# The last attention group of a hybrid decoder trunk in another order: output projections ahead of the new rows' steps, first normalisation chunk ahead of the last heads' work

## The reference, cut to what matters

```python
# layer 0, for the 1024 prompt rows and the 8 sample rows
q, k, v = split(x @ w_qkv); q, k = rope(q), rope(k)
s = q k^T / 8, window of 128 back, with one sink per head
o = softmax_with_sink(s) v
x = layer_norm(ALPHA * x + o @ w_o, ln_mix_g[0], ln_mix_b[0])
u = x @ ffn_w_in[0]                      # and so on: the FFN of layer 0
# layer_norm: mu = mean(x); var = mean((x - mu)^2)
#             (x - mu) * rsqrt(var + eps) * g + b
```

## Time and profile before

| | |
|---|---|
| median of three runs | 2870.3 us (2869.7 to 2871.86) |
| the profiled execution's own time | 2871.64 us |
| its span, first to last instruction | 2869.8 us |
| PE busy | 2810.4 us (98%) |
| DVE, ACT, POOL busy | 1482.6, 899.0, 579.8 us |
| mean granted TensorE clock | 0.991 of full |

### The profile page before, as it was taken

How to read it: one execution, slowest core, us unless ns; L and a number is a source line. 1 busy time by engine, 2 the same in 40 slices (tenths; PEclk the granted TensorE clock), 3 DMA queues, 4 the chain that set the end, 5 groups by cost and what they waited for, 6 DMA issues and landing times.

```text
span 2869.8 us, 44638 instructions
## 1 busy us (share of the span) xinstructions
PE 2810.4 (98%) x18308; PEld 2704.3 (94%) x18308; DVE 1482.6 (52%) x2974; ACT 899.0 (31%) x1690; POOL 579.8 (20%) x505
## 2 busy tenths in 40 slices
PE   8999989999999999999999999999999999999996
PEld 7888879999999999999999999899999999999996
DVE  6556576444444444714445454365765444444446
ACT  5445454221111122422343433422252221222223
POOL 3334351000000002402223232111330000000004
PEclk9999999999999999999999999999999999999998
DMA  4210111111111112234566665776402111111101
GB/s 134 79 46 17 30 46 45 45 45 45 52 52 45 45 45 65 68 114 147 187 192 198 184 191 180 245 244 191 139 30 74 45 45 58 46 45 45 45 25 59
DMA packets 193434, 260.51 MB, mean 91 GB/s; under 512 B 29200, under 2 KB 151696, under 8 KB 193200
## 3 DMA queue, kind: packets, MB, share of 16 engines
q1 hardware_dynamic: 128336, 196.16, 21.8%
q10 hardware_dynamic: 64896, 61.50, 6.3%
HBM read 191.50 MB, written 68.20 MB: 90 GB/s over the span
## 4 chain that ended last, share of the span: by engine, by line
PE 91%; DVE 4%; ACT 2%; issue 1%; POOL 1%; DMA 1%; SPq 0%; ACTq 0%; DVEq 0%; POOLq 0%
PE bank L493 28%; PE bank L495 28%; PE bank L494 28%; PE bank L628 1%; PE bank L650 1%; ACT y L1046 1%; PE bank L955 1%; PE bank L908 1%; PE bank L640 0%; PE bank L917 0%; DVE bank L1525 0%; PE bank L902 0%; DMA xl<-scratch_heads_lo 0%; PE bank L605 0%; ACT xh L1050 0%
## 5 line engine op out<-in xcount | busy, mean ns | idle before, releaser
L493 PE MATMUL bank<-xh,wh 128*128 128x344 f32 x3600 | 1162.2, 323 | 6.5 <-DMA xl<-scratch_heads_lo 4.0
L495 PE MATMUL bank<-xh,wl 128*128 128x344 f32 x3600 | 1152.2, 320 | 0.0
L494 PE MATMUL bank<-xl,wh 128*128 128x344 f32 x3600 | 1151.4, 320 | 0.0
L493 PEld LDWEIGHTS bank<-xh,wh 128*128 128x128 f32 x3600 | 678.1, 188 | 21.9 <-issue 14.1
L494 PEld LDWEIGHTS bank<-xl,wh 128*128 128x128 f32 x3600 | 677.6, 188 | 4.8
L495 PEld LDWEIGHTS bank<-xh,wl 128*128 128x128 f32 x3600 | 678.3, 188 | 0.0
L1503 DVE TENSOR_TENSOR y<-bank,y 128x344 f32<-128x344 f32 x576 | 290.1, 514 | 219.4 <-PE bank L495 218.8
L2156 POOL TENSOR_TENSOR f_hl<-f_cv,f_hh 128x344 fp32r<-128x344 f32 x132 | 123.0, 932 | 1265.6 <-ACT f_hh L1198 1265.6
L493 PE MATMUL bank<-f_hh,wh 128*128 128x344 f32 x1056 | 340.2, 322 | 0.0
L495 PE MATMUL bank<-f_hh,wl 128*128 128x344 f32 x1056 | 337.7, 320 | 0.0
L494 PE MATMUL bank<-f_hl,wh 128*128 128x344 f32 x1056 | 337.4, 320 | 0.0
(11 more groups left out here) (230 smaller groups left out, 3417.3 us busy)
## 6 DMA issues: line engine op xcount, KB each, us to landing
raw<-in_w SPq DMA_DIRECT2D x216, 512.0 KB, 3.7
scratch_qkvg<-p_plain ACTq DMA_DIRECT2D x96, 172.0 KB, 2.8
r_s<-in_state_in SPq DMA_DIRECT2D x32, 512.0 KB, 3.7
out_state_s<-r_s ACTq DMA_DIRECT2D x32, 512.0 KB, 5.7
scratch_qkvg<-p_rot ACTq DMA_DIRECT2D x24, 344.0 KB, 3.1
xh<-scratch_heads_hi SPq DMA_DIRECT2D x12, 688.0 KB, 8.9
xl<-scratch_heads_lo SPq DMA_DIRECT2D x12, 688.0 KB, 10.4
r_cxq<-scratch_qkvg SPq DMA_DIRECT2D x32, 256.0 KB, 5.7
```

Of the source, the lines that this page charges most:

```text
L493: pe.matmul(out, ah, bh, start=(k == 0), stop=False)
L494: pe.matmul(out, ah, bl, start=False, stop=False)
L495: mm = pe.matmul(out, al, bh, start=False, stop=(k == n - 1))
```

## The change

In the last group only:

- PE: jobs 0 to 3 are issued in the loop ahead of the sample rows' projection (`project(8)`), jobs 4 and 5 between `turn(7)` and `values(4)`, jobs 6 and 7 ahead of `turn(8)`. `mean(0)` stands ahead of job 8, `var(0)` behind job 13, `mean(1)` still behind job 19.
- DVE: `centre(0)`, `sum2(0)`, `inverse_root(0)`, `scale(0)` move ahead of the last `inverse`, of `heads_lo(6)`, of `sample_probs_copy` and of `heads_lo(7)`; the adds follow the jobs.
- ACT: `squares(0)` moves ahead of `heads_hi(6)`; a one-element Sqrt behind `sample_exp` loads the table early; `root(0)` comes ahead of the slabs' splits; `normal(0, ...)` stands inside the group, around `sample_heads_hi`. The order of slab splits is now: 20 behind `root(0)`, 21 behind `heads_hi(7)`, 22 and 23 behind `normal(0, 1)`.
- POOL: the sums of chunk 0 go between the `probs`; its queue behind that is as before.
- The PSUM banks of the jobs from 8 on are 0, 1 and 3 in turn; the sample rows' scores move from bank 3 to bank 4. In SBUF a gap of 1152 words a partition moves ahead of `a_t1` to behind `a_t2`, so that the squares and sums lie free of them.

```diff
@@ def job_order() @@
-        jobs += [("qkv", g, b) for b in range(NB + 1)] + [("ao", g, q) for q in range(24)]
+        n = 4 if g == NG - 1 else 0
+        jobs += [("qkv", g, b) for b in range(NB)] + [("ao", g, q) for q in range(n)]
+        jobs += [("qkv", g, NB)] + [("ao", g, q) for q in range(n, 24)]
@@ PSUM bank of job q @@
+    if q < 8:
+        return q % 2
+    return (0, 1, 3)[(q - 8) % 3] if g == NG - 1 else (0, 1, 3, 4)[q % 4]
@@ tensor_engine: project, down @@
+            if last and b == NB:
+                pe.wait_ge(S["yadd"], 24 * g + 3)
...
+                if last and q in (0, 1, 4):
+                    pe.wait_ge(T["rope_t"], (NB + 1) * g + (NB + 1 if q == 4 else NB - 1 + q))
+                if last and q == 10:
+                    pe.wait_ge(S["n_cent"], 1)
@@ tensor_engine: attention @@
                 turn(t - 1)
+            if last and t == NB:
+                down(4, 6)
             if t >= 4:
                 values(t - 4)
             if t >= 3:
                 turn_probs(t - 3)
+            if last and t == NB - 1:
+                down(0, 4)
+        if last:
+            down(6, 8)
+            turn(NB)
+            values(NB - 3)
+            scores(NB - 1)
+            turn_probs(NB - 2)
+            pe.wait_ge(T["shifted"], GH * NB * (g + 1))
+            mean(0)
+            down(8, 10)
+            sample_scores()
+            values(NB - 2)
+            sample_turn()
+            down(10, 12)
+            turn_probs(NB - 1)
+            down(12, 14)
+            var(0)
+            values(NB - 1)
+            sample_turn_probs()
+            down(14, 16)
+            sample_values()
+            down(16, 20)
+            mean(1)
+            down(20, 24)
+            return
@@ scalar_engine: attention @@
+            if last and t == NB + 1:
+                pt_in(t - 3)
             if t >= 2:
                 exps(t - 2)
-            if t >= 3:
+            if t >= 3 and not (last and t == NB + 1):
                 pt_in(t - 3)
...
         if last:
+            act.wait_ge(T["expd"], NB * (g + 1))
             squares(0)
+            heads_hi(NB - 2)
+            sample_exp()
+            act.activation(K.warm[:, :], K.eps[:, :], ACT.Sqrt)
+            pt_in(NB - 1)
+            act.wait_ge(S["g_in"], 64)
+            root(0)
             split_next(1)
+            heads_hi(NB - 1)
+            split_next(1)
+            normal(0, 0)
+            sample_heads_hi()
+            normal(0, 1)
+            split_next(2)
@@ scalar_engine, behind the groups @@
-    act.wait_ge(S["g_in"], 64)
-    root(0)
-    normal(0, 0)
-    normal(0, 1)
     squares(1)
@@ vector_engine: attention @@
+            if last and t == NB - 1:
+                add_y(0, 4)
+        if last:
+            add_y(4, 6)
+            inverse(NB - 2)
+            add_y(6, 8)
+            t_lo(NB)
+            heads_lo(NB - 3)
+            shift(NB - 1)
+            centre(0)
+            inverse(NB - 1)
+            add_y(8, 10)
+            sample_copy()
+            sample_shift()
+            sum2(0)
+            add_y(10, 12)
+            heads_lo(NB - 2)
+            sample_probs()
+            add_y(12, 13)
+            inverse_root(0)
+            scale(0)
+            sample_probs_copy()
+            heads_lo(NB - 1)
+            add_y(13, 16)
+            sample_heads()
+            sample_heads_lo()
+            normal_lo(0, (0,))
+            add_y(16, 18)
+            normal_lo(0, (1,))
+            add_y(18, 20)
+            centre(1)
+            add_y(20, 24)
+            sum2(1)
+            return
@@ pool_engine: attention @@
             if t >= 3:
+                if t == NB + 1 and g == NG - 1:
+                    sums(key, 0, 0, 4, 6)
                 if t == NB + 2 and g == NG - 1:
-                    sums(key, 0, 0, 1, 4)
+                    sums(key, 0, 0, 6, KT)
                 probs(t - 3)
             if t <= NB:
                 add_rope(t)
+            if t == NB and g == NG - 1:
+                sums(key, 0, 0, 1, 4)
         if g < NG - 1:
...
         else:
-            sums(key, 0, 0, 4, KT)
             for s in range(20, 23):
                 split_lo(s)
             sums(key, 0, 1, 1, KT)
```

More of the change, by code:

```diff
@@ L201, with att_bank @@
 EV = evac_table()
+def att_bank(g, q):
+    if q < 8:
+        return q % 2
+    return (0, 1, 3)[(q - 8) % 3] if g == NG - 1 else (0, 1, 3, 4)[q % 4]
 def bank_table():
@@ L208, in bank_table @@
         kind = key[0]
-        if kind == "qkv" or (kind == "ao" and key[1:] < (NG - 1, 16)):
+        if kind == "qkv" or (kind == "ao" and key[1:] < (NG - 1, 8)):
             continue
         if kind == "ao":
-            b = (0, 1, 5)[key[2] % 3]
+            b = att_bank(key[1], key[2])
         elif kind == "up":
@@ L309, in last_columns @@
     return slice(2 * CH + part.start, 2 * CH + part.stop), part
[L312 to L316, removed]
 def att_before(g, q):
@@ L404, in build @@
         K.same = sb("same", [32, NS])
-        sb("a_gap", [P, 1152])
         K.a_t1 = sb("a_t1", [P, 2, 320])
         K.a_t2 = sb("a_t2", [P, 2, 320])
+        sb("a_gap", [P, 1152])
         K.a_sm = sb("a_sm", [P, GH, 2 * W])
@@ L659, in sample_scores @@
             for b in range(NS):
-                pe.matmul(bank[3][:, b:32:NS], K.a_kc[:, b, :], K.a_sq[:, 0:4, b], start=True, stop=True)
-            pe.matmul(bank[4][0:32, 0:NS], K.a_sq[:, 0:4, :], K.a_sq[:, 4, :], start=True, stop=True).then_inc(T["s_sc"], 1)
+                pe.matmul(bank[4][:, b:32:NS], K.a_kc[:, b, :], K.a_sq[:, 0:4, b], start=True, stop=True)
+            pe.matmul(bank[4][0:32, 32:32 + NS], K.a_sq[:, 0:4, :], K.a_sq[:, 4, :], start=True, stop=True).then_inc(T["s_sc"], 1)
         def sample_turn():
@@ L720, in attention @@
         sample_turn()
-        if last:
-            mean(0)
         down(8, 12)
@@ L727, in attention @@
         sample_values()
[L728 to L735, removed]
+        down(14, 24)
     def ffn_up(L, t, kind, ch):
@@ L1154, in attention, with sample_exp, sample_heads_hi @@
         act.dma_start(A["vwin_s"][:, W - 1, g, :], K.a_vs[:, :]).then_inc(T["kv_out"], 16)
[L1155 to L1165, removed]
+        def sample_exp():
+            act.wait_ge(T["s_mx"], 3 * g + 3)
+            act.activation(K.a_sp[:, :], bank[2][0:32, 0:W + 1], ACT.Exp, bias=K.a_sst[:, 2:3], scale=HD ** -0.5,
+                           accum_out=K.a_sst[:, 4:5])
+            act.activation(K.a_sst[:, 5:6], K.a_sst[:, 3:4], ACT.Exp).then_inc(T["s_ex"], 1)
+        def sample_heads_hi():
+            act.wait_ge(T["s_of"], 2 * g + 2)
+            act.activation(K.a_oh[:, :, SEQ:TOK], K.a_of[:, :, :], ACT.Copy).then_inc(T["s_oh"], 1)
         if last:
+            act.wait_ge(T["expd"], NB * (g + 1))
             squares(0)
-        act.wait_ge(T["s_of"], 2 * g + 2)
-        act.activation(K.a_oh[:, :, SEQ:TOK], K.a_of[:, :, :], ACT.Copy).then_inc(T["s_oh"], 1)
-        if last:
-            split_next(1)
-        else:
+            heads_hi(NB - 2)
[4 more added lines that the diff above has]
+            root(0)
+            split_next(1)
+            heads_hi(NB - 1)
[4 more added lines that the diff above has]
+            split_next(2)
+        else:
+            split_next(1)
+            heads_hi(NB - 2)
+            pt_in(NB - 1)
+            split_next(1)
+            sample_exp()
+            heads_hi(NB - 1)
+            split_next(1)
+            sample_heads_hi()
             act.wait_ge(S["jobs"], J["ao", g, 23])
@@ L1617, in sample_copy @@
             dve.wait_ge(T["s_sc"], g + 1)
-            dve.tensor_copy(K.a_ss[:, :], bank[3][:, 0:32]).then_inc(T["s_scc"], 1)
-            dve.tensor_tensor(K.a_new[:, 0:NS], bank[4][0:32, 0:NS], K.same[:, :], ALU.mult).then_inc(T["s_scc"], 1)
+            dve.tensor_copy(K.a_ss[:, :], bank[4][:, 0:32]).then_inc(T["s_scc"], 1)
+            dve.tensor_tensor(K.a_new[:, 0:NS], bank[4][0:32, 32:32 + NS], K.same[:, :], ALU.mult).then_inc(T["s_scc"], 1)
             dve.wait_ge(T["s_scc"], 3 * g + 2)
@@ L1693, in attention @@
         add_y(10, 12)
-        if last:
-            centre(0)
         heads_lo(NB - 1)
@@ L1700, in attention @@
         sample_heads_lo()
[L1701 to L1714, removed]
+        add_y(14, 24)
     def conv(L, t, ch):
```

## The result

The changed kernel takes 2874.26 us (median of 18 runs, 2872.25 to 2876.66), the kernel before 2870.23 (18 runs beside them): a ratio of 1.0015, 95% interval 1.0009 to 1.0021. It is 4.0 us slower, inside the range and within 0.2%, but on the slower side of no change: the interval excludes one. The prediction had 2871.7.

A forecast was written before the change was run, and what follows sets the result against it. PE, busy 98% of the span, was taken as the bound, with some 20 us winnable at most. Earlier chunk 0 work, offset by a new wait at mean(1), left var(1) 1.4 later: 2870.3 + 1.4 = 2871.7 us, range 2866.0 to 2878.0.

The forecast's parts named there:

- The bound, the place and the mechanism: PE-bound; at mean(1), PE waits 7 to 10 us for POOL's sums, held behind slab 22's split after normal(0,1).
- The early part: Last group up to mean(0): two new PE waits of 1.7 us each, yet mean(0) at 368.0 against 371.93.
- wait 1.1 us at job 13: Chunk 0: job 13 waits about 1.1 us for add 10, behind sum2, before var(0) runs to 380.65.
- wait 2.7 for the copy and 2.0 for the sample heads: Ahead of job 16, PE waits for DVE's steps behind scale(0); job 16 starts at 390.3.
- The new wait's size: At mean(1): slab 22's low part ends at 397.1, seven sums take 7.2; PE waits 7 to 10 us.
- the contention of the two engines: At sum2(1): DVE and POOL share SBUF interfaces, so 3.6 us; without it, var(1) ready 1.1 us sooner on DVE's side.
- From mean(1) to var(1): Half to all of jobs 20 to 23 run at low clock; FFN starts 411.4 to 412.8, var(1) 415.2 to 416.6.
- the +1.4: At var(1): it comes at 415.9 against 414.47, 1.4 us later, and the end moves by as much.
- no idle time that matters: PE behind the FFN's first var, in the kernel before: nothing there changes, so the end moves as var(1) does.
- The faster one: Wait at mean(1) absent or short: var(1) at about 408, 6.5 us sooner, 2863.8 us; chance 0.10.
- The slower one: Clock low for over 11 us after the wait at mean(1): 6.4 us, 2876.7 us; chance 0.15.
- The parts that I costed at nothing: Table load behind sample_exp, banks 0, 1, 3, the moved SBUF gap, slab loads, stores: no cost, apart from waits at jobs 13 and 23.

The follow-up runs named there:

- POOL's order: Changed kernel with POOL's sums of chunk 1 moved ahead of the low part of slab 22: 2864.72 us, ratio 0.9982 to the kernel before.
- ACT's order: Changed kernel with ACT splitting slab 22 right behind slab 21, ahead of normal(0,0): 2867.82 us, ratio 0.9994 to the kernel before.
- the cause alone: Kernel before with only ACT's splits of slabs 22 and 23 moved behind normal(0,1): 2886.77 us in one execution.
- the run with the extra matmuls: Changed kernel with 48 unread matmuls into free bank 7 ahead of mean(1), keeping PE busy: 2871.11 us, ratio 1.0004 to the kernel before.
- the first experiment: Changed kernel with POOL's sums of chunk 1 moved ahead of slab 22's low part: 2864.72 us, ratio 0.9982 to the kernel before.
- taking the 0.70 away: Changed kernel with POOL's chunk 1 sums ahead of slab 22, plus banks 1, 0, 3 in turn from job 8: 2864.77 us.
- the first try for a better order: The reordered-sums kernel with banks 1, 0, 3, plus sample rows' steps ahead of scale(0) and normal(0,0), and POOL's sums split: 2865.54 us, ratio 0.9989.
- the run of the table load: Kernel before with only a one-element Sqrt added behind sample_exp, loading the table early: 2870.04 us, ratio 1.0001.

## Why the prediction was right

**The bound, the place and the mechanism** were as put: mean(1) after 9.65 us of idle time that POOL ended (6 to 11 forecast), POOL idle 7.50 us ahead of its third low part (over 6), mean(0) and var(0) 3.4 and 10.3 us sooner, no table load ahead of the root, var(1) at 418.08, 0.1 outside the 413 to 418 I gave. POOL's order, ACT's order and the cause alone (9.5 and 6.4 us less than the changed kernel, 16.8 more than before) show the mechanism from both sides.

**The early part.** New waits of 1.67 and 1.91 for the 1.7 and 1.7 forecast. One step failed: I let jobs 10 to 13 run at full clock and had PE wait 1.1 us at job 13. The window at 374 us has the clock at 0.57 with no wait in it, behind the two short waits; what brings it the last section takes up. PE itself was late, there was no wait, and var(0) came at 380.81 for my 379.2. Some 0.4 of that is where the trace begins, the rest the clock. Ahead of job 16 I had PE wait 2.7 for the copy and 2.0 for the sample heads; it was 2.89 and 0.96, the matmuls of `sample_values` between them having run at the low clock (1.87 us, at full clock 1.10). The wait at mean(1) covers both.

**The new wait's size.** I had mean(1) at 404.5, it came at 406.62. Of these 2.1 us, 1.3 were there when POOL started on slab 22 (396.00 for my 394.7) and are var(0)'s, handed down the chain. The rest is slab 22's low part, 3.33 us where I took 2.36: it ran beside DVE's normal_lo, and I had applied the contention of the two engines to DVE's sum2(1) only, not to POOL. The seven sums took 7.2, as put.

**From mean(1) to var(1).** Jobs 20 to 23 were low for about two thirds of their time (to 411.6), between my half and all; the FFN started 7.61 behind mean(1) (6.9 to 8.3), its wait for job 23's add was 0.70, and var(1) had no wait. sum2(1), with POOL at the sums of chunk 2, took 3.44 us (1.95 and 1.49) for my 3.6. So the +1.4 became +3.6 by two terms of the sum: var(0) late by the clock, and POOL slowed by DVE. Behind var(1) nothing moved in this profile, as I had it. But I had read more into the kernel before than its trace holds when I wrote that it shows no idle time that matters there. PE waits 4.02 us in layer 1, with the low clock behind it (0.50 over 1852 to 1856 us), and 7.8 in the last norm:

```profile
1853.41 0.63 PE L493 MATMUL bank<-xh,wh 128*128 128x344 f32 x1 [4.02 <-DMA xl<-scratch_heads_lo]
```

In the changed kernel the two are 3.85 and 7.8, so they cancel between these two profiles. For the first that was luck: in the run with the extra matmuls it is 2.59, and the stretch is 3.7 us shorter, more than the +1.4 that I forecast.

**The rivals.** The faster one (no wait at mean(1), 2863.8) priced a kernel that wasn't this one, and the first experiment is that kernel: 2864.72. The slower one, the low clock for over 11 us, didn't come: 5.0 us, and not even the 5.9 of the kernel before, which I had taken for the least behind a longer wait. Most of the 2.6 us that the median lies above my 2871.7 is in the two terms just named.

**The parts that I costed at nothing.** The table load in its new place holds up nothing: pt_in(7) behind it starts at 378.92, after an idle time of 1.02. The banks cost a wait of 0.70 at the FFN's start, which the sum had, and not the one at job 13; with POOL's order repaired, taking the 0.70 away gave nothing.

## What to carry to other kernels

When steps are moved ahead on one engine, follow every instruction that they pass on its way to the other engines: a weight split that nobody wanted for 20 us was the lock in front of a queue that the next normalisation needed. The repair was to turn two items of POOL's queue, not to take the change back. A wait taken away from an in-order engine is worth only what the next wait doesn't take, so read the last one ahead of the stretch where the engine runs full. Where two engines slow each other, as DVE and POOL do here, look for each moved step at what the other one does at that time.

## What the runs showed of the hardware that I had not expected

**VectorE and GpSimd slow each other both ways.** An fp32 operation of two SBUF inputs, 128x1376, took DVE 1.59 us alone, 1.58 to 2.29 beside POOL's sums, and up to 3.73 beside POOL's slab splits; POOL's split took 2.36 alone and up to 3.7. In the first try for a better order this ate most of what PE had won. The rows look less like a slower pace than like one engine waiting for the other's instruction to end. In the kernel before, an addition of 32x1 in SBUF took DVE 1.59 us and ended with POOL's splits (372.01 and 4.72); the same in the changed kernel, with POOL idle, took 0.15:

```profile
375.15 1.59 DVE L1636 TENSOR_TENSOR a_sst<-a_sst 32x1 f32<-32x1 f32 x1
```

```profile
379.85 0.15 DVE L1678 TENSOR_TENSOR a_sst<-a_sst 32x1 f32<-32x1 f32 x1
```

And where DVE's normal_lo had begun first, at 395.55, it took its usual 1.58 us to 397.13, and it was POOL's split, begun at 396.00, that was 1.0 us longer.

**One far wait decides some 3 us of a profile.** In layer 1 PE waits once for heads read back from memory, 2.6 to 5.2 us in the twelve profiles. In the changed kernel, after 3.85 us, the clock falls behind it; in the run with the extra matmuls, after 2.59, it doesn't. The windows of PE, the changed kernel first, then that run:

```profile
1852.00:1856.00 4.00, 0.42 (x4) 0.93 1.02 379
1856.00:1860.00 4.00, 3.73 (x13) 0.50 0.96 343
1860.00:1864.00 4.00, 4.00 (x23) 0.71 1.07 392
```

```profile
1852.00:1856.00 4.00, 3.18 (x20) 1.00 1.01 375
1856.00:1860.00 4.00, 4.00 (x29) 1.00 1.08 395
1860.00:1864.00 4.00, 4.00 (x27) 1.00 1.06 381
```

That is 3.7 us between two profiles, with no edit near it. In the other ten the wait was 3.15 us or more, and the clock fell behind it in each. It may be why executions of one kernel scatter over some 4 us; only the profiled ones show it, so this isn't settled.

**The same short waits are followed by a fall of the clock in one profile and not in another.** In the changed kernel PE ran at half rate from 374.1 to 377.5 us (0.57 in the window), busy throughout, with waits of 1.67 and 1.91 us at job 6 and at mean(0) ahead of it. But how long the waits are doesn't say where the clock falls. The windows of PE behind job 6, where both runs had waited 1.7 us, in the changed kernel and in the run with the extra matmuls, which has the same program up to there:

```profile
360.00:364.00 4.00, 2.33 (x21) 1.00 0.00 0
```

```profile
360.00:364.00 4.00, 4.00 (x24) 0.61 0.02 4
```

And the kernel before and the run of the table load, again the same program up to there, with waits of 0.52 and 0.7 us since 350 in both:

```profile
368.00:370.00 2.00, 1.89 (x27) 1.00 0.00 0
```

```profile
368.00:370.00 2.00, 2.00 (x25) 0.65 0.00 0
```

Such a stretch cost PE 1 to 3 us in these profiles. Nothing in the rows told where it would come, so a forecast of this kind of change should leave room for it, and so should the reading of a single profile.
